# Four modulation vectors summed on VectorE in 128 half chunks; the first gather between expert steps

## The chip, the cores and the metric

The kernel runs on one core of a Trainium2 chip. The time is the device time of one execution in microseconds. Before the change three runs gave a median of 3161.8 us (3160.68 to 3172.74).

## The reference

Two transformer blocks over 256 tokens of width 2048, batch 1, all in float32. Only the first touches the change:

```python
c_act = jax.nn.silu(c)
mod = c_act @ w_ada[l] + b_ada[l]                      # [1, 6 * 2048]
shift1, scale1, gate1, shift2, scale2, gate2 = jnp.split(mod, 6, axis=-1)
h = modulate(rms_norm(x, norm_mix_g[l]), shift1, scale1)
...                                                    # y_sb, y_s5, y_ml: three branches of h
merged = sigmoid(g_sb) * (y_sb @ p_sb) + sigmoid(g_s5) * (y_s5 @ p_s5) + sigmoid(g_ml) * (y_ml @ p_ml)
x = x + gate1[:, None, :] * (merged @ w_out[l])
h = modulate(rms_norm(x, norm_moe_g[l]), shift2, scale2)
x = x + gate2[:, None, :] * hierarchical_moe(h, ...)   # 32 experts, 2 per token
```

The six vectors of 2048 are products of one row, c_act, with a 2048 x 12288 matrix: 96 MB are read for them, and each element is used once. shift1 and scale1 are wanted first of all, gate1 at w_out, shift2 and scale2 after it, gate2 in the experts. The second block (three branches, gates, an output projection) has no such vectors.

## The kernel before

**Chunks.** Weights come in chunks of 128 x 2048 floats (1 MB) from a list `main` of 317, in the order of `PHASES`: p_sb, g_sb, glu, g_sb2, p_s5, g_s5, mlif, ml, p_ml, g_ml, wout, router, then the second block's, which ends in g_c, wout2, ple and pgate. SyncE's queue loads chunk n into one of four slots of `stage`. ScalarE copies it, rounded, to `w_hi` (`high`, line 1302 on), GpSimd subtracts to get `w_lo` (`low`, line 542 on, four instructions of 512 columns, two buffers, so at most two chunks ahead of TensorE), and TensorE forms x_hi w_hi + x_lo w_hi + x_hi w_lo in one of four PSUM banks of `acc`. A chunk of a gate stage (g_*) is `both`: 16 matmuls over 512 columns and 16 over 256; one of a p stage or glu is `half`, one of wout `deep`. ScalarE's `step` waits for the chunk, evacuates it and makes the w_hi four chunks on. In a gate stage the evacuation is a sum of two halves on VectorE, a sigmoid on ScalarE, then one or two multiplications and additions on VectorE (`merge_g`).

**The modulation vectors.** The first two are made at the start (`ada_part`, 32 chunks through `stage`). The other four, numbered u = 0 to 3, ride along: the chunks of `ada` are loaded by ScalarE's queue into one `side_buf` of 1 MB (`side_load`), and after each chunk of g_sb, g_sb2 (u = 0), g_s5 (1), g_ml (2) and wout (3) TensorE waits for the side chunk and multiplies it with c_act as weights: four matmuls of 32 x 512 in four row groups (`side`, `beside_ada`), accumulating in banks 2 or 3 of `wk`. ScalarE loads the next when `side_used` says that this one is done (`side_next`). After 16 chunks it copies 512 columns to `side_row`, TensorE turns them into columns with four matmuls (`ada_columns`), and VectorE adds the bias (`modulation`). An fp32 matmul is two load and two matmul records in the trace.

**The experts.** 192 chunks of 1 MB go through a ring of 8 slots. TensorE gathers the tokens of the first eight teams' slots with 16 tiles of products (`gather(0, ...)`, four matmuls a tile, two PSUM banks), which ScalarE copies to `xg` and `xgo` (`rows_in`), and waits for all 16. Only then comes the first `up_step`, which uses tiles 0 to 3 and ring slots of four experts and gives these back; `up_step(0, c)` uses tiles 4c to 4c + 3.

Everything is in order on its engine, and engines wait for one another by semaphores only.

Of the kernel before, what the change touches and what calls it, by code (L numbers as in the profile page):

```python
# [22 lines left out]
P = 128  # L23
# [70 lines left out]
for _name, _n in VECS:  # L94
    VC[_name] = NV
    NV += _n


def slot(a, i=0, per=1):

    return a % 4, a // 4 + i * per


def build(nc, dr):
# [183 lines left out]
    side_in = nc.alloc_semaphore("side_in")  # L288
# [276 lines left out]
    def _(pe):  # L565
# [171 lines left out]

        def beside_ada(name, u, step, t0=0, n=16):
            for t in range(n):
                k, q = slot(BASE[name] + t)  # L740
                step(k, q)
                side(u, t0 + t)
# [72 lines left out]
        beside_ada("g_sb", 0, both, 0, 8)  # L815
# [190 lines left out]
        gather(0, range(DT))  # L1006
        for d in range(TRIPLES):
            a, b, o = 3 * d, 3 * d + 1, 3 * d + 2
            pe.wait_ge(xg_ready, DT * (d + 1))
            if d:  # L1010
                pe.wait_ge(hid_ready, a - 1)
            up_step(a, 0)
            if d:
                combine(b - 3)
            up_step(a, 1)
            if d:
                down_step(o - 3, 0)
            up_step(a, 2)
            if d:
                down_step(o - 3, 1)  # L1020
            up_step(a, 3)
            if d:
# [270 lines left out]
    def _(act):  # L1293
        def fn(o, i, f, **kw):
            return act.activation(o, i, f, **kw)  # L1295
# [42 lines left out]
        def side_load(u, t):  # L1338
            act.dma_start(side_buf[u][:], dr["ada"][NADA + u * 16 + t]).then_inc(side_in, 16)

        def side_next(u, t):
            act.wait_ge(side_used, u * 16 + t + 1)
            if t < 15:
                side_load(u, t + 1)
            else:
                fn(side_row[u][:], wk[:, 2 + u % 2, :], ACT.Copy).then_inc(row_ready, 1)
# [95 lines left out]
        def merge_p(p, pt):  # L1442
            def go(k, q, t):
                step(k, q, lambda: fn(pt[:, ds(t * 2, 2), :] if not isinstance(t, int) else pt[:, 2 * t:2 * t + 2, :],
                                      acc[:, k, :], ACT.Copy).then_inc(evac_done, 1))
            each(act, BASE[p], 8, go)

        def merge_g(g, sg, b2=None, u=None, t0=0, n=16):
# [8 lines left out]
            if u is None:  # L1457
                each(act, BASE[g], 16, go)
            else:
                for t in range(t0, t0 + n):  # L1460
                    go(*slot(BASE[g] + t - t0), t)
                    side_next(u, t)
            sg_n[0] += n

        act.wait_ge(y5_ready, 9)
        side_load(0, 0)
# [4 lines left out]
        merge_g("g_sb", A["sg"], u=0, n=8)  # L1471
        for t in range(4):
            k, q = slot(BASE["glu"] + t)
            if t >= 2:
                act.wait_ge(glu_ready, t - 1)
            step(k, q, to(A["y5sg"][:, t % 2, :], k, ACT.Sigmoid, 2))
        act.wait_ge(glu_ready, 4)
        fn(yh[:], A["y5"][:], ACT.Copy).then_inc(gelu_done, 1)
        merge_g("g_sb2", A["sg"], u=0, t0=8, n=8)
        act.wait_ge(sg_used, 16)  # L1480
        merge_p("p_s5", ptmp1)
        act.wait_ge(ada_sum, 3)
        side_load(1, 0)
        merge_g("g_s5", A["sg"], u=1)


# [52 lines left out]
        side_load(2, 0)  # L1539
        merge_p("p_ml", ptmp1)  # L1540
        merge_g("g_ml", B["sg"], u=2)
        side_load(3, 0)
# [10 lines left out]
        for t in range(16):  # L1553
            wout_step(*slot(BASE["wout"] + t), t, t < 13)
            side_next(3, t)
# [298 lines left out]
    def _(dve):  # L1854
        def tt(o, a, b, op):
            return dve.tensor_tensor(o, a, b, op)  # L1856
# [228 lines left out]

        def merge_g(g, sg, pt, first=False, t0=0, n=16):
# [4 lines left out]
            def go(k, q, t):  # L2091
# [3 lines left out]
                tt(sg[:, k % 2, :], sg[:, k % 2, :], acc[:, k, T:2 * T], ADD).then_inc(sg_sum, 1)  # L2095
                dve.wait_ge(evac_done, q * 4 + k + 1)
# [7 lines left out]
            if n < 16:  # L2104
                for t in range(t0, t0 + n):
                    go(*slot(BASE[g] + t - t0), t)
            else:
                each(dve, BASE[g], 16, go)
            if not first:
                sg_n[0] += 16  # L2110

        dve.wait_ge(gelu_done, 2)
        tt(yl[:], A["y5"][:], yh[:].bitcast(F32), SUB).then_inc(y_split, 1)
        merge_g("g_sb", A["sg"], ptmp1, True, 0, 8)
        for t in range(4):
            dve.wait_ge(evac_done, BASE["glu"] + t + 1)
            o = A["y5"][:, 2 * t:2 * t + 2, :]
            tt(o, o, A["y5sg"][:, t % 2, :].rearrange("p (c t) -> p c t", c=2), MUL).then_inc(glu_ready, 1)
        dve.wait_ge(gelu_done, 3)
        tt(yl[:], A["y5"][:], yh[:].bitcast(F32), SUB).then_inc(y_split, 1)  # L2120
        merge_g("g_sb2", A["sg"], ptmp1, True, 8, 8)
        modulation(2)
        merge_g("g_s5", A["sg"], ptmp1)
# [84 lines left out]
        stage_b(None, 3)  # L2208
        merge_g("g_ml", B["sg"], ptmp1)
# [13 lines left out]
        modulation(4)  # L2223
        dve.wait_ge(mod_ready, 5)
        stt(a2[:], mod[:, 64:80], 1.0, vec[:, VC["g_moe"]:VC["g_moe"] + 16], ADD, MUL).then_inc(mod_ready, 1)
        each(dve, BASE["wout"], 16, add_out)
# [687 lines left out]
```

## Time and profile before

| | us |
|---|---|
| median of three runs | 3161.8 |
| lowest and highest | 3160.68, 3172.74 |
| the profiled execution's own time | 3177.29 |
| its span, first to last instruction | 3175.4 |
| TensorE, VectorE, ScalarE, GpSimd busy | 2880.4, 1291.5, 1189.0, 1687.4 |

The profile is one execution. Its rows give, by engine or group, the busy time, the mean of one instruction, and how long the engine stood idle before it and for whom. PE is TensorE's matmuls, PEld its weight loads, DVE VectorE, ACT ScalarE, POOL GpSimd, SPq and ACTq the queues from which DMAs are issued.

### The profile page before, as it was taken

What the parts mean: (1) busy time and instruction counts of PE and PEld (TensorE: products, weight loads), DVE (VectorE), ACT (ScalarE), POOL (GpSimd) and SP (SyncE); (2) the same over time, 40 slices, a digit from 0 to 9 for tenths busy, and PEclk for the clock granted to TensorE, in tenths of its full rate; (3) what the DMA queues carried; (4) which work ended last, traced back from release to release, by engine and by line L of the source; (5) the groups of instructions that cost most, each with busy time, mean ns of one, the idle gap of its engine ahead of it and who ended that gap; (6) DMA issues with size and microseconds to landing.
All of it is one profiled execution on the core that took longest, in us unless ns stands there. A gap on an engine that the chain in (4) does not pass through costs nothing.

```text
span 3175.4 us, 51257 instructions
## 1 busy us (share of the span) xinstructions
PE 2880.4 (91%) x19812; PEld 2380.7 (75%) x19812; DVE 1291.5 (41%) x2025; ACT 1189.0 (37%) x1457; POOL 1687.4 (53%) x1274
## 2 busy tenths in 40 slices
PE   6899989999999999858788879889999999999998
PEld 1688777787998778733343338789988989998998
DVE  1488833224544252331222224247723253315344
ACT  1233343333454432321011104556744446644344
POOL 0000067777785875400000004967779997779798
PEclk8999989999999999979998988999999999999999
DMA  9533336667343686549999972534445554435443
GB/s 390 207 129 114 124 133 252 240 253 279 136 162 127 229 299 243 215 186 397 421 397 392 397 310 89 190 138 142 151 146 185 185 189 159 158 144 188 162 165 141
DMA packets 98628, 679.76 MB, mean 214 GB/s; under 512 B 11584, under 2 KB 15424, under 8 KB 16832
## 3 DMA queue, kind: packets, MB, share of 16 engines
q1 hardware_dynamic: 83088, 602.97, 50.3%
q10 hardware_dynamic: 15408, 74.85, 6.4%
q8 instruction: 105, 1.72, 0.2%
q14 instruction: 27, 0.22, 0.0%
HBM read 770.05 MB, written 2.10 MB: 243 GB/s over the span
## 4 chain that ended last, share of the span: by engine, by line
PE 54%; DMA 9%; POOL 4%; DVE 3%; issue 3%; ACT 2%; SPq 1%; ACTq 0%; POOLq 0%; DVEq 0%
PE acc L567 33%; PE wk L567 7%; PE acc L640 7%; DMA ring<-in_moe 6%; POOL w_lo L549 4%; PE acc L644 4%; DMA side_buf<-in_ada 2%; PE acc L653 2%; SPq L499 1%; ACT w_hi L1295 1%; DMA stage<-in_main 1%; DVE hb L1856 0%; DVE dl L1856 0%; ACT L1295 0%; ACT hb L1295 0%
## 5 line engine op out<-in xcount | busy, mean ns | idle before, releaser
L549 POOL TENSOR_TENSOR w_lo<-stage,w_hi 128x512 fp32r<-128x512 f32 x1268 | 1680.2, 1359 | 1439.6 <-ACT w_hi L1295 958.5
L1295 ACT ACTIVATE w_hi<-stage 128x2048 fp32r<-128x2048 f32 x317 | 604.0, 1907 | 49.1 <-DMA stage<-in_main 48.8
L567 PE MATMUL acc<-xhl,w_hi 128*128 128x256 f32 x4064 | 523.7, 287 | 20.9 <-DVE xhl L1856 10.0
L567 PEld LDWEIGHTS acc<-xhl,w_hi 128*128 128x128 f32 x4064 | 507.1, 195 | 24.9 <-DVE xhl L1856 7.5
L640 PE MATMUL acc<-xhl,w_hi 128*128 128x512 f32 x1536 | 373.7, 396 | 0.0
L640 PEld LDWEIGHTS acc<-xhl,w_hi 128*128 128x128 f32 x1536 | 283.5, 189 | 93.9 <-issue 36.7
L567 PE MATMUL acc<-xhl,w_lo 128*128 128x256 f32 x2032 | 271.5, 287 | 2.0 <-POOL w_lo L549 2.0
L567 PEld LDWEIGHTS acc<-xhl,w_lo 128*128 128x128 f32 x2032 | 256.3, 194 | 5.4 <-issue 2.5
L567 PE MATMUL acc<-h,stage 128*128 128x256 f32 x1024 | 234.8, 385 | 2.9 <-ACT h L1295 2.9
L567 PEld LDWEIGHTS acc<-h,stage 128*128 128x128 f32 x1024 | 193.0, 191 | 40.3 <-issue 15.1
L644 PEld LDWEIGHTS acc<-xhl,w_lo 128*128 128x128 f32 x1536 | 196.9, 191 | 7.5
L644 PE MATMUL acc<-xhl,w_lo 128*128 128x256 f32 x1536 | 199.1, 283 | 0.0
L1295 ACT ACT_TABLE_LOAD x136 | 174.5, 1283 | 50.9 <-DVE G_sg L1856 27.4
L567 PE MATMUL acc<-ring,xg 128*32 128x512 f32 x1024 | 135.3, 673 | 51.1 <-DMA ring<-in_moe 49.2
L1862 DVE SCALAR_TENSOR_TENSOR x<-wk,mod,x 128x256 f32<-128x256 f32 x192 | 82.4, 480 | 185.6 <-PE wk L567 185.5
L567 PEld LDWEIGHTS acc<-ring,xg 128*32 128x32 f32 x1024 | 36.4, 121 | 140.5 <-issue 136.0
L567 PE MATMUL acc<-yh,w_hi 128*128 128x256 f32 x576 | 139.8, 281 | 0.0
L567 PE MATMUL acc<-yl,w_hi 128*128 128x256 f32 x576 | 139.6, 281 | 0.0
L567 PE MATMUL acc<-dh,w_hi 128*128 128x256 f32 x512 | 126.8, 288 | 6.4 <-DVE dl L1856 6.4
L1295 ACT ACTIVATE X_ysb<-wk 128x2048 f32<-128x2048 f32 (+1 forms) x12 | 22.5, 1878 | 283.6 <-PE wk L567 187.7
L567 PE MATMUL acc<-dl,w_hi 128*128 128x256 f32 x512 | 124.9, 284 | 0.0
L567 PEld LDWEIGHTS acc<-dh,w_hi 128*128 128x128 f32 x512 | 98.2, 192 | 19.3 <-issue 16.2
(486 smaller groups left out, 4021.6 us busy)
## 6 DMA issues: line engine op xcount, KB each, us to landing
stage<-in_main SPq DMA_DIRECT2D x317, 1024.0 KB, 4.8
ring<-in_moe SPq DMA_DIRECT2D x192, 1024.0 KB, 10.6
side_buf<-in_ada ACTq DMA_DIRECT2D x64, 1024.0 KB, 5.0
over_lo<-in_moe ACTq DMA_DIRECT2D x48, 1024.0 KB
over_hi<-in_moe ACTq DMA_DIRECT2D x42, 1024.0 KB
stage<-in_ada SPq DMA_DIRECT2D x32, 1024.0 KB, 8.6
stage<-in_sb SPq DMA_DIRECT2D x32, 1024.0 KB, 4.8
x<-in_x ACTq DMA_DIRECT2D x1, 2048.0 KB, 12.9
```

Of the source, the lines that this page charges most:

```text
L499: sp.dma_start(ring[:, r, :], dr["moe"][tile * 6 + c]).then_inc(ring_in[r], 16)
L549: last = pool.tensor_tensor(w_lo[:, k % 2, cs], stage[:, k, cs], w_hi[:, k, cs].bitcast(F32), ALU.subtract)
L567: return pe.matmul(o, w, r, start=start, stop=stop)
L640: pe.matmul(acc[:, k, :], w_hi[:, k, t * P:(t + 1) * P], xhl[:, :, t, :], start=t == 0, stop=False, skip_group_check=True)
L644: last = pe.matmul(acc[:, k, 0:T], w_lo[:, k % 2, t * P:(t + 1) * P], xh[:, t, :], start=False, stop=t == DT - 1, skip_group_check=True)
L653: return pe.matmul(o, w, r, start=start, stop=stop, skip_group_check=True)
L1295: return act.activation(o, i, f, **kw)
L1862: return dve.scalar_tensor_tensor(out=o, in0=a, scalar=s, in1=b, op0=op0, op1=op1)
```

## The change

The four side vectors leave TensorE. Each `ada` chunk is loaded as two halves of 128 x 1024 floats (512 KB) into two buffers, and VectorE multiplies a half with c_act's column (a scalar per partition) and adds it to 1024 columns of `wk` in PSUM (`side_sum`), 128 times. `SIDE` says how many halves go with each chunk of each stage: 32 for each vector, u = 0 over p_sb to g_sb2, 1 over p_s5 and g_s5, 2 over p_ml and the first eight of g_ml, 3 over the last four of g_ml and wout. After the 32nd, ScalarE copies all 2048 columns, and TensorE sums over the partitions with 16 matmuls of 128 x 128 weights by one column of ones (`side_columns`), after the first chunk of p_s5, after mlif, after the tenth chunk of g_ml and after wout. In the expert stage the first gather's tiles 8 to 11 stand behind tiles 0 to 7 and the first up_step, tiles 12 to 15 behind the second. In the diff the three engines' parts are put under their names.

```diff
+SIDE = {"p_sb": (1, 1, 2, 1, 2, 1, 2, 2), "g_sb": (1,) * 8, "glu": (1,) * 4, "g_sb2": (1,) * 8,
+        "p_s5": (0, 0, 2, 2, 2, 2, 2, 2), "g_s5": (2, 1, 1, 1) * 4,
+        "p_ml": (2,) * 8, "g_ml": (2,) * 8 + (0, 0, 0, 0, 1, 2, 1, 2), "wout": (2,) * 12 + (1, 1, 0, 0)}
...
+def side_halves(name, t):
+    return range(SIDE_FROM[name][t], SIDE_FROM[name][t + 1])
...
-    side_at = [S0 + 14336, S0 + 14336, S0 + 12288, XH0]
-    side_buf = [sb(f"side_buf{u}", [P, CH], at=at) for u, at in enumerate(side_at)]
-    side_row = [sb(f"side_row{u}", [P, 512], at=at) for u, at in enumerate(side_at)]
+    side_at = [S0 + 14336, S0 + 14336, S0 + 12288, S0 + 12288]
+    side_buf = [sb(f"side_buf{u}", [P, 2, CH // 2], at=at) for u, at in enumerate(side_at)]
+    side_row = [sb(f"side_row{u}", [P, CH], at=at) for u, at in enumerate(side_at)]
...
@@ TensorE
-        def side(u, t):
-            pe.wait_ge(side_in, 16 * (u * 16 + t) + 16)
-            ada_part(side_buf[u], t, 2 + u % 2).then_inc(side_used, 1)
+        def side_columns(u):
+            v = 2 + u
+            pe.wait_ge(row_ready, v + 1)
+            for b in range(16):
+                last = mm(wk[:, 1, v * 16 + b:v * 16 + b + 1], side_row[u][:, b * P:(b + 1) * P], ones[:, 0:1])
+            last.then_inc(ada_sum, 1)
...
-        beside_ada("g_sb2", 0, both, 8, 8)
+        each(pe, BASE["g_sb2"], 8, both)
         pe.wait_ge(y_split, 2)
-        each(pe, BASE["p_s5"], 8, half)
-        ada_columns(2, side_row[0])
-        beside_ada("g_s5", 1, both)
+        half(*slot(BASE["p_s5"]))
+        side_columns(0)
+        for t in range(1, 8):
+            half(*slot(BASE["p_s5"] + t))
+        each(pe, BASE["g_s5"], 16, both)
         each(pe, BASE["mlif"], 1, wide)
-        ada_columns(3, side_row[1])
+        side_columns(1)
...
-        beside_ada("g_ml", 2, both)
+        for t in range(16):
+            both(*slot(BASE["g_ml"] + t))
+            if t == 9:
+                side_columns(2)
...
             deep(*slot(BASE["wout"] + t))
-            if t == 1:
-                ada_columns(4, side_row[2])
-            side(3, t)
-        ada_columns(5, side_row[3])
+        side_columns(3)
...
-        gather(0, range(DT))
+        for c in range(4):
+            gather(0, range(4 * c, 4 * c + 4))
+            if c:
+                pe.wait_ge(xg_ready, 4 * c)
+                up_step(0, c - 1)
+        pe.wait_ge(xg_ready, DT)
+        up_step(0, 3)
...
@@ ScalarE
+        def side_load(n):
+            b, cs = n % 2, slice(n % 2 * (CH // 2), (n % 2 + 1) * (CH // 2))
+            act.dma_start(side_buf[n // 32][:, b, :], dr["ada"][NADA + n // 2][:, cs]).then_inc(side_in[b], 16)
+        def side_first(u):
+            for b in range(2):
+                side_load(u * 32 + b)
+        def side_next(name, t):
+            for n in side_halves(name, t):
+                act.wait_ge(side_used, n + 1)
+                if n % 32 < 30:
+                    side_load(n + 2)
+                if n % 32 == 31:
+                    fn(side_row[n // 32][:], wk[:, :, :].rearrange("p a b -> p (a b)"), ACT.Copy).then_inc(row_ready, 1)
...
@@ VectorE
+        def side_sum(name, t):
+            for n in side_halves(name, t):
+                b = n % 2
+                o = wk[:, 2 * b:2 * b + 2, :].rearrange("p a b -> p (a b)")
+                c = cact[:, n // 2 % 16:n // 2 % 16 + 1]
+                dve.wait_ge(side_in[b], 16 * (n // 2) + 16)
+                if n % 32 < 2:
+                    if n >= 32:
+                        dve.wait_ge(mod_ready, n // 32 + 2)
+                    ts(o, side_buf[n // 32][:, b, :], c, MUL).then_inc(side_used, 1)
+                else:
+                    dve.wait_ge(side_used, n - 1)
+                    stt(o, side_buf[n // 32][:, b, :], c, o, MUL, ADD).then_inc(side_used, 1)
...
                 tt(sg[:, k % 2, :], sg[:, k % 2, :], acc[:, k, T:2 * T], ADD).then_inc(sg_sum, 1)
+                if g in SIDE:
+                    side_sum(g, t - t0)
                 dve.wait_ge(evac_done, q * 4 + k + 1)
```

In p_sb, glu, p_s5, p_ml and wout `side_sum` and `side_next` are called after each chunk in the same way; `modulation(4)` and `a2` move from before wout to after the tenth g_ml chunk, `side_first(1)` waits for the columns of vector 0, and `side_first(3)` for those of vector 2.

## Rows read from the trace of the kernel before

**Rows 1.** The page: busy time and share of each engine.
```profile
PE 2880.4 (91%) x19812; PEld 2380.7 (75%) x19812; DVE 1291.5 (41%) x2025; ACT 1189.0 (37%) x1457; POOL 1687.4 (53%) x1274
```

**Rows 2.** Busy time by stretch (columns in the first row): two of block one, one of block two.
```profile
core 0: us, PE busy (x) PEld busy (x) DVE busy (x) ACT busy (x) POOL busy (x), PEclk, DMA share, GB/s
466.69:770.72 304.03, 287.88 (x1868) 235.43 (x1870) 95.36 (x112) 109.33 (x94) 235.47 (x176) 0.98 0.70 256
1067.27:1305.06 237.79, 228.10 (x1599) 187.33 (x1597) 79.64 (x82) 72.39 (x66) 169.33 (x129) 0.99 0.75 275
2859.52:3052.05 192.53, 189.09 (x1363) 178.59 (x1362) 76.28 (x81) 78.37 (x69) 169.30 (x128) 1.00 0.50 176
```

**Rows 3.** The same of g_s5, g_b and p_b; then groups by line in g_s5.
```profile
656.40:763.10 106.70, 100.33 (x608) 77.98 (x606) 46.20 (x54) 33.74 (x30) 80.27 (x61) 1.00 0.79 286
2500.50:2584.10 83.60, 83.60 (x498) 74.51 (x497) 43.93 (x53) 34.96 (x30) 80.62 (x61) 1.00 0.53 188
2455.00:2494.70 39.70, 39.70 (x323) 39.05 (x322) 4.05 (x6) 16.66 (x14) 35.68 (x28) 1.00 0.51 186
...
L549 POOL TENSOR_TENSOR w_lo<-stage,w_hi 128x512 fp32r<-128x512 f32 x61 | 81.5, 1367 | 27.0 <-PE acc L644 25.7 <-PE acc L567 1.3
...
L640 PEld LDWEIGHTS acc<-xhl,w_hi 128*128 128x128 f32 x224 | 41.0, 188 | 19.0 <-issue 10.9
```

**Rows 4.** The tile side_buf: duration min/median/max, waits for it, landing.
```profile
L567 PE MATMUL wk<-side_buf,cact x512: 592/616/1062, 477.8 to 1313.1; 128*32 128x512 f32 x171
L1339 ACTq DMA_DIRECT2D side_buf<-in_ada x64: 334/334/357, 432.3 to 1306.9; - x64
...
  DMA side_buf<-in_ada: 52.0, 44
...
DMA to landing us min/median/max: 4.6/5.0/7.6
```

**Rows 5.** Timeline at the end of wout: start, length, engine, operation, [idle before].
```profile
1314.44 0.97 PEld L567 LDWEIGHTS wk<-ident,side_row 128*128 128x128 f32 x8 [1.62 <-ACT side_row L1295]
...
1315.32 6.78 PEld L567 LDWEIGHTS acc<-ident,ones 128*128 128x128 f32 x60
...
1325.50 0.30 PEld L567 LDWEIGHTS wk<-rms_red,ones 128*128 128x128 f32 x2 [3.40 <-DVE rms_red L1868]
```

**Rows 6.** Groups by line and shape: VectorE's, then ScalarE's from the page.
```profile
L1862 DVE SCALAR_TENSOR_TENSOR x<-wk,mod,x 128x256 f32<-128x256 f32 x192 | 82.4, 480 | 185.6 <-PE wk L567 185.5
...
L1856 DVE TENSOR_TENSOR A_sg<-A_sg,ptmp 128x256 f32<-128x256 f32 x16 | 22.0, 1374 | 10.5 <-ACT A_sg L1295 10.5
...
L1856 DVE TENSOR_TENSOR merged<-merged,A_sg 128x256 f32 x16 | 21.0, 1311 | 2.0
...
L1856 DVE TENSOR_TENSOR A_sg<-A_sg,acc 128x256 f32<-128x256 f32 x32 | 13.5, 421 | 1.1
...
L1856 DVE TENSOR_TENSOR x<-x,R_ot 128x256 f32 x16 | 16.9, 1059 | 82.5 <-ACT R_ot L1295 82.5
...
L1856 DVE TENSOR_TENSOR hb<-x,rinv 128x1024 f32<-128x1024 f32 x8 | 9.3, 1220 | 0.1
L1856 DVE TENSOR_TENSOR hb<-merged,rinv 128x1024 f32<-128x1024 f32 x4 | 9.1, 2340 | 0.0
...
L1295 ACT ACTIVATE w_hi<-stage 128x2048 fp32r<-128x2048 f32 x317 | 604.0, 1907 | 49.1 <-DMA stage<-in_main 48.8
```

**Rows 7.** DMA issues between 1290 and 1450 us: count, KB each, median us to landing.
```profile
R_iota<-in_iota ACTq DMA_DIRECT2D x1, 128.0 KB, 2.2
```

**Rows 8.** Timeline of the first gather and expert steps; a stretch of the expert stage.
```profile
1384.03 0.38 ACT L1295 ACTIVATE xg<-acc 128x256 f32<-128x256 f32 x1 [0.17 <-PE acc L567]
...
1391.08 0.16 PEld L567 LDWEIGHTS acc<-ring,xg 128*32 128x32 f32 x8 [0.96 <-ACT xgo L1295]
...
1394.79 40.45 SPq L499 DMA_DIRECT2D ring<-in_moe  x20
...
1450.00:1550.00 100.00, 86.08 (x623) 41.72 (x616) 23.14 (x64) 15.41 (x38) 0.00 (x0) 0.97 0.98 402
```

More of the change, by code:

```diff
@@ L96 @@
     NV += _n
+SIDE = {"p_sb": (1, 1, 2, 1, 2, 1, 2, 2), "g_sb": (1,) * 8, "glu": (1,) * 4, "g_sb2": (1,) * 8,
+        "p_s5": (0, 0, 2, 2, 2, 2, 2, 2), "g_s5": (2, 1, 1, 1) * 4,
+        "p_ml": (2,) * 8, "g_ml": (2,) * 8 + (0, 0, 0, 0, 1, 2, 1, 2), "wout": (2,) * 12 + (1, 1, 0, 0)}
+SIDE_FROM, _n = {}, 0
+for _name, _per in SIDE.items():
+    SIDE_FROM[_name] = [_n + sum(_per[:j]) for j in range(len(_per) + 1)]
+    _n += sum(_per)
+assert _n == 128
+def side_halves(name, t):
+    return range(SIDE_FROM[name][t], SIDE_FROM[name][t + 1])
 def slot(a, i=0, per=1):
@@ L287, in build @@
     ada_used = nc.alloc_semaphore("ada_used")
-    side_in = nc.alloc_semaphore("side_in")
+    side_in = [nc.alloc_semaphore(f"side_in{b}") for b in range(2)]
     side_used = nc.alloc_semaphore("side_used")
@@ L736, in _ @@
         ada_columns(1, ada_row[:, 1, :])
[L738 to L742, printed above, removed]
         def stage_a(g, s):
@@ L1445, in go, with merge_g @@
                                       acc[:, k, :], ACT.Copy).then_inc(evac_done, 1))
-            each(act, BASE[p], 8, go)
-        def merge_g(g, sg, b2=None, u=None, t0=0, n=16):
+            if p not in SIDE:
+                each(act, BASE[p], 8, go)
+                return
+            for t in range(8):
+                go(*slot(BASE[p] + t), t)
+                if t == 1 and p == "p_s5":
+                    act.wait_ge(ada_sum, 3)
+                    side_first(1)
+                side_next(p, t)
+        def merge_g(g, sg, b2=None, t0=0, n=16):
             n0 = sg_n[0] - t0
@@ L1456, in go @@
                 step(k, q, evac)
-            if u is None:
+            if g not in SIDE:
                 each(act, BASE[g], 16, go)
             else:
-                for t in range(t0, t0 + n):
-                    go(*slot(BASE[g] + t - t0), t)
-                    side_next(u, t)
+                for t in range(n):
+                    go(*slot(BASE[g] + t), t0 + t)
+                    side_next(g, t)
+                    if t == 10 and g == "g_ml":
+                        act.wait_ge(ada_sum, 5)
+                        side_first(3)
             sg_n[0] += n
         act.wait_ge(y5_ready, 9)
-        side_load(0, 0)
+        side_first(0)
         merge_p("p_sb", ptmp1)
@@ L1470, in _ @@
         fn(yh[:], A["y5"][:], ACT.Copy).then_inc(gelu_done, 1)
-        merge_g("g_sb", A["sg"], u=0, n=8)
+        merge_g("g_sb", A["sg"], n=8)
         for t in range(4):
@@ L1538, in _ @@
         act.wait_ge(by_ready, 4)
-        side_load(2, 0)
+        side_first(2)
         merge_p("p_ml", ptmp1)
-        merge_g("g_ml", B["sg"], u=2)
-        side_load(3, 0)
+        merge_g("g_ml", B["sg"])
         def wout_step(k, q, t, more=True):
@@ L1554, in _ @@
             wout_step(*slot(BASE["wout"] + t), t, t < 13)
-            side_next(3, t)
+            side_next("wout", t)
         rms_root(2)
@@ L2102, in go @@
                     tt(merged[:, t, :], merged[:, t, :], sg[:, k % 2, :], ADD).then_inc(sg_used, 1)
-            if n < 16:
-                for t in range(t0, t0 + n):
-                    go(*slot(BASE[g] + t - t0), t)
+            if g in SIDE:
+                for t in range(n):
+                    go(*slot(BASE[g] + t), t0 + t)
+                    if t == 9 and g == "g_ml":
+                        modulation(4)
+                        scale2()
             else:
@@ L2110, in merge_g @@
                 sg_n[0] += 16
+        for t in range(8):
+            side_sum("p_sb", t)
         dve.wait_ge(gelu_done, 2)
@@ L2118, in _ @@
             tt(o, o, A["y5sg"][:, t % 2, :].rearrange("p (c t) -> p c t", c=2), MUL).then_inc(glu_ready, 1)
+            side_sum("glu", t)
         dve.wait_ge(gelu_done, 3)
@@ L2122, in _ @@
         modulation(2)
+        for t in range(8):
+            side_sum("p_s5", t)
         merge_g("g_s5", A["sg"], ptmp1)
@@ L2208, in _ @@
         stage_b(None, 3)
+        for t in range(8):
+            side_sum("p_ml", t)
         merge_g("g_ml", B["sg"], ptmp1)
@@ L2222, in _ @@
         split_merged(1)
[L2223 to L2226, printed above, removed]
+        for t in range(16):
+            add_out(*slot(BASE["wout"] + t), t)
+            side_sum("wout", t)
         dve.wait_ge(ot_used, 16)
```

34 lines of the change are left out of this document (12 added, 22 removed).

## The prediction, made before the change was run

> **What bounds the kernel now.** I read the first part of the page, then the stretches of the two blocks side by side, then the side buffer's tile, then the groups of VectorE. TensorE is busy for 91% of the span, GpSimd for 53%, VectorE for 41% [rows 1]; work that stays beside TensorE costs time only where it delays it. The second block does the work of the first without side chunks, so it shows what the first could cost. One chunk is four w_lo instructions on GpSimd, so the instruction counts of a stretch count its chunks. The first block's 44 chunks from g_sb to the end of g_s5 took 304.0 us (x176), its g_ml and wout 237.8 us (x129, 32 chunks); the second block's g_c and wout2, the same 32 chunks, took 192.5 us (x128) [rows 2]. In g_b 15 chunks take 83.6 us, 5.57 each, TensorE busy throughout and GpSimd for 80.6 us of it; in p_b 7 half chunks take 39.7 us, 5.67 each. In g_s5 the same 15 chunks take 106.7 us, 7.11 each, at the full clock: 1.54 us more per chunk. TensorE and GpSimd are both near the limit at 5.57: GpSimd in g_s5 idles for 27.0 us, waiting for TensorE [rows 3].
>
> The 1.54 us are the side step: its matmuls (8 records a chunk of 616 ns median, four at a time, about 1.1 us), 52.0 us of idle time waiting for the one side buffer (44 times), and a gap of issue behind each, 10.9 us in g_s5 alone [rows 3, 4].
>
> **Part 1, the matmuls leave TensorE.** If the g and wout stages fall to the second block's pace: 32 gate chunks x 5.573 + 12 half chunks x 5.671 = 246.4 us in place of 304.0, a gain of 57.6; g_ml and wout 192.5 in place of 237.8, a gain of 45.3. The small transposes of ada_columns (0.97 us each [rows 5]) are in these stretches twice and go with them; the third, after mlif, goes against its replacement.
>
> **Part 2, the column sums.** Each of four vectors now wants 16 matmuls of 128x128 weights by one column, in place of 4. One fp32 matmul is two records: the 4 gave x8 loads in 0.97 us, and 60 loads of the same kind took 6.78 us, 0.12 each [rows 5]. So 32 x 0.12 = 3.9 us per vector; the upper bound is 6.1, if each load stood alone for 0.19. Three lie on TensorE in stretches that it bounds: 3.9 behind the first p_s5 chunk, 3.9 in g_ml, 3.9 - 1.0 = 2.9 behind mlif. The fourth stands before the spinning matmuls at the end of wout, where TensorE then waits 3.4 us for the squares [rows 5]; it costs nothing there. The row copies grow from 512 to 2048 columns (1.9 us by the w_hi copy, as long [rows 6]); ScalarE makes each one chunk or more before TensorE asks. Two waits are new: after the tenth g_ml chunk VectorE (modulation(4)) and, one chunk on, ScalarE (its next side load) wait for the column sums. Behind them stand the copies and the evacuation of the chunk that TensorE begins only then, 5.6 us before they are due. After g_s5 both engines waited for mod in the same places before. SP's and GpSimd's programs don't change.
>
> **Part 3, the sums on VectorE.** 128 instructions over 1024 columns, SBUF and PSUM in, PSUM out. No such row exists. Nearest below: PSUM and SBUF in with a pointer scalar, 256 columns, 480 ns; with 1.04 ns per further column (421 ns at 256, 1220 at 1024) this gives 1.28 us. Upper bound: operations with two SBUF inputs are stretched beside a working GpSimd, at 1024 columns from 1220 to 2340 ns, at 256 from 421 to about 1374. With one input in PSUM they stay at 421 beside the same GpSimd [rows 6], so I take 1.28 and keep 2.34 for the range. Lower bound: 1.22.
> The Trainium skill, "SBUF — State Buffer", section "SBUF: two separate sides", has a lock behind this: a VectorE operation with two SBUF inputs and a GpSimd operation exclude one another for whole instructions. By its rule the new sums, with one SBUF input, are free of it; the trace agrees for SBUF output (421 against 1374 ns), and none here writes PSUM.
> VectorE per chunk of g_s5 is 0.42 + 0.42 + 1.37 + 1.31 = 3.5 us [rows 6]; with 1.25 sums on average 5.1, below 5.57. In wout 1.06 + 2.56 = 3.6 against 6.5. In the first eight g_ml chunks, two sums each, it is 6.1, with gaps about 6.4 against 5.57: VectorE falls 0.8 behind per chunk, 6.4 us in all, then catches up in the four chunks without sums. What waits for it is ScalarE's sigmoid, then the next w_hi behind it on ScalarE; GpSimd asks for that w_hi two chunks later (11.1 us), so about 8 us of lateness cost nothing. But p_ml already hands over some. I charge half, 3 us.
>
> **Part 4, the side loads.** 128 loads of 512 KB in two buffers in place of 64 of 1024 KB in one, each issued by ScalarE (0.33 us) after the sum that frees its buffer. Landing: 128 KB took 2.2 us, 1024 KB 5.0 (4.6 to 7.6) [rows 4, 7]; in between, 3.4. A loop of sum, issue and landing is 1.28 + 0.35 + 3.4 = 5.0 us, and a chunk with two halves uses each buffer once: 5.0 to 5.6 per chunk. This just fits under 5.57. Behind the wait for the sum on ScalarE stand the next evacuation and w_hi (1.9 us [rows 6]), both inside the landing time. Of the first eight g_ml chunks this asks 2 MB per 5.57 us, 376 GB/s; g_s5 ran at 286 GB/s with a DMA share of 0.79 [rows 3], the experts at 402 with 0.98 [rows 8]. It is close to full for 36 chunks at most. I charge nothing beyond the 3 us, and keep the rest for the rival.
> The Trainium skill, "DMA: Bandwidth & Descriptors", section "Bandwidth", wants transfers of at least 1 MiB, since each pays a fixed part of about 2 us ("Anatomy of one DMA"): halving pays that twice. As an estimate from this page a half is 2.0 + 1.2 = 3.2 us, the loop 4.8, and the sum stays. It speaks against the change only if the loop, not TensorE, is the bound; the trace's 2.2 us for 128 KB agrees with a fixed part of about that size.
> In p_sb (12 halves), p_s5 (12) and p_ml (16) VectorE has almost nothing else, and ScalarE's step, mostly its w_hi, fits in the landing time. At the end of p_sb the last two sums come before ScalarE's Gelu and the split: about 2 us later, and the first gate chunk's w_hi with it. I charge 2.
>
> **Part 5, the first gather.** The expert stage is a stream of DMA, 0.98 of the engines, and it starts when the first expert step gives its four ring slots back. The eighth tile's gather was copied at 1384.03; the first expert matmul started at 1391.08 behind the sixteenth, and the first refill was issued at 1394.79, 3.7 us later [rows 8]. Now the step starts behind the eighth gather: 1383.95 + 3.7 = 1387.7, 7.1 us earlier. The second step (four gathers at half of 1391.08 - 1384.03, 3.5 us, and 3.7 for itself) ends by 1394.9, before the four new chunks have landed (10 us at 402 GB/s), so the stream has no hole, and the whole of it moves forward by 7.1. Bounds: 4 us if the second step left a hole of 3, 8 if the two gathers ran at the faster pace of the later ones. pick_rows(1) and the first over_load move later by two steps and by the code are wanted only behind the fourth.
>
> **The sum.** 57.6 - 3.9 + 45.3 - 3.9 - 2.9 + 7.1 = 99.3. Less 3 (VectorE in g_ml), 2 (Gelu), and 2.5 because the stretches with a mean clock of 0.98 and 0.99 may keep half of their slow part, which the second block's do not have: 92. The profiled execution took 3177.3 us, so 3085 in its own time; the median of the runs is 15.5 below it, so 3161.8 - 92 = 3070.
>
> **Rivals.**
> A, VectorE becomes the bound: the sums take 2.34 us, as two SBUF inputs would. For it: no row writes PSUM from VectorE. g_s5 is then 3.5 + 2.9 + gaps = 6.75 per chunk (+1.2 x 16 = 19), g_ml's first eight 8.5 (+23), its last four +7, p stages +8: the gain falls by 57 to 35, 3127.
> B, the side loop is the bound: under load a half lands in 6 us, as whole ones did at 7.6 at worst [rows 4]. A two-half chunk is then 7.7 us: p_s5 +12, p_ml +9, g_ml +17, wout +15 = 53, gain 39, 3123. For it the 376 GB/s; against it the median of 5.0 for twice the bytes.
> C, slower: each sum holds GpSimd off for its whole length. Place: the w_lo instructions, of which four take 4 x 1.367 = 5.5 us of a chunk's 5.57 [rows 3], so nothing hides it. 128 x 1.28 = 164 us against the 99 gained: 3161.8 + 65 = 3227. It decides from 99 / 128 = 0.78 us per sum. Against it: the 421 ns rows, where nobody waited.
> D, the pace of the first block has another cause than the side step and stays near 6.9: then only the gather and a few us of waits remain, 3150. Against it: the same chunks at 5.57.
>
> **Chances.** Forecast 0.64 (its own range 3052 to 3092), A 0.08, B 0.15, D 0.06, C 0.07. A change of 0.5% (16 us) is what a measurement of this kernel can tell from none. The forecast, A and B are faster: 0.87; D is the same: 0.06; C slower: 0.07. The range 3048 to 3128 holds the forecast, A and B.
>
> **What would show it.** Right: g_s5 and g_ml near 5.6 us per chunk and wout near 6.5, the sums at about 1.28 us, w_lo still at 1.37, side_columns at about 3.9, the halves landing in 3.4 to 4.5, the first refill 3.7 us behind the eighth gather. Wrong: w_lo waiting for ScalarE or running over 1.5 us, sums over 2 us, or VectorE waiting for the side loads in most two-half chunks.

## The result, and the profile after

The changed kernel took 3133.3 us (median of five runs, 3129.39 to 3143.89), the kernel before 3162.6 beside it: a ratio of 0.9898, 95% interval 0.9883 to 0.9914. It is faster by 29 us; 92 were forecast and the forecast was 3070. Rival B, the side loop bound by its landings, had given 3123.

The page's first row and the two stretches of [rows 2] in the kernel after (columns as there). The first stretch runs again from the first w_lo of g_sb to that of mlif, the second from the first of g_ml to the router's:

```profile
PE 2828.8 (90%) x19396; PEld 2393.7 (76%) x19396; DVE 1415.8 (45%) x2153; ACT 1194.6 (38%) x1457; POOL 1679.5 (54%) x1274
```

```profile
466.04:723.92 257.88, 254.92 (x1654) 233.93 (x1653) 142.63 (x164) 113.21 (x95) 231.96 (x176) 0.99 0.83 290
1024.33:1261.30 236.97, 207.53 (x1408) 192.31 (x1407) 129.06 (x134) 75.79 (x66) 165.77 (x129) 0.94 0.75 261
...
1024.33:1145.85 121.52, 100.64 (x543) 87.01 (x542) 72.80 (x85) 41.48 (x36) 84.16 (x64) 0.90 0.72 252
1145.85:1261.30 115.45, 106.89 (x867) 105.29 (x866) 56.27 (x50) 34.31 (x30) 81.61 (x65) 0.97 0.78 270
```

The same change, two answers. The first stretch fell from 304.0 us to 257.9 [rows 2], most of what was forecast. The second stayed: 237.8 to 237.0. TensorE is busy there for 20 us less than before (207.5 against 228.1), and the time went into idling: g_ml alone grew from 111.6 to 121.5, with 20.9 us of TensorE idle in it and a granted clock of 0.90. Against the 92.8 us that the same 16 chunks took without most of the side loads (experiment 3) it is 28.8 longer: 20.9 of idle time, and 7.9 of busy time more (100.6 against 92.8) at the lower grant. The first stretch asks for one half beside most chunks; p_ml, the first eight chunks of g_ml and twelve of wout ask for two.

What was late? The tile side_buf after the change, with how long VectorE stood for its loads, who then stood for VectorE, and the landings (compare [rows 4]):

```profile
L1357 ACTq DMA_DIRECT2D side_buf<-in_ada x128: 334/334/528, 431.7 to 1258.5; - x128
...
  DMA side_buf<-in_ada: 181.3, 72
...
  ACT R_ot L1312: 54.4, 11
  ACT ptmp L1312: 53.5, 11
...
DMA to landing us min/median/max: 3.8/5.6/10.2
```

A half of 512 KB landed in 5.6 us (median), where 1024 KB had taken 5.0 [rows 4] and the forecast had 3.4. Half the bytes did not come sooner. The loads of `stage` took longer too: between the first w_lo of g_ml and the router's their median was 6.8 us, in the kernel before 4.8. VectorE waited for 72 of the 128 halves. Neither VectorE's work nor GpSimd's was the trouble, as the groups by line show (the sums; the w_lo copies, 1367 ns in g_s5 in [rows 3]):

```profile
L1894 DVE SCALAR_TENSOR_TENSOR wk<-side_buf,cact,wk 128x1024 f32<-128x1024 f32 x120 | 154.1, 1287 | 161.9 <-DMA side_buf<-in_ada 161.6
...
L564 POOL TENSOR_TENSOR w_lo<-stage,w_hi 128x512 fp32r<-128x512 f32 x1268 | 1672.3, 1352 | 1399.2 <-ACT w_hi L1312 1001.7
```

How a late half reaches TensorE is seen in one chunk of g_ml, in the timeline of VectorE, of ScalarE and its queue, and of GpSimd (start, length, engine, operation, idle before and for whom):

```profile
1057.47 1.29 DVE L1894 SCALAR_TENSOR_TENSOR wk<-side_buf,cact,wk 128x1024 f32<-128x1024 f32 x1 [5.09 <-DMA side_buf<-in_ada]
...
1060.79 0.42 DVE L1888 TENSOR_TENSOR B_sg<-B_sg,acc 128x256 f32<-128x256 f32 x1
...
1063.03 1.29 DVE L1894 SCALAR_TENSOR_TENSOR wk<-side_buf,cact,wk 128x1024 f32<-128x1024 f32 x1 [0.63 <-DMA side_buf<-in_ada]
...
1058.79 0.33 ACTq L1357 DMA_DIRECT2D side_buf<-in_ada  x1
1061.30 0.42 ACT L1312 ACTIVATE B_sg<-B_sg 128x256 f32<-128x256 f32 x1 [6.70 <-DVE B_sg L1888]
1061.62 1.90 ACT L1312 ACTIVATE w_hi<-stage 128x2048 fp32r<-128x2048 f32 x1
...
1063.59 5.38 POOL L564 TENSOR_TENSOR w_lo<-stage,w_hi 128x512 fp32r<-128x512 f32 x4 [3.92 <-ACT w_hi L1312]
```

VectorE stands 5.09 us for a half. Behind that sum, in order, are the four small operations that give ScalarE the next gate's sum; ScalarE had idled for 6.70 us, then makes the w_hi, and GpSimd, idle for 3.92, follows. The load issued at 1058.79 is used at 1063.03, 4.2 us later, and only when that sum is done can the buffer's next load start. The waits of that stretch, and what TensorE stood for:

```profile
ACT B_sg L1312 <- DVE B_sg L1888: 56.5, 13, 10.6
DVE wk L1894 <- DMA side_buf<-in_ada: 32.2, 17, 5.2
POOL w_lo L564 <- ACT w_hi L1312: 25.8, 11, 6.1
...
PE wk L582 <- ACT side_row L1312: 10.7, 1, 10.7
```

The last row is one wait: after its tenth g_ml chunk TensorE asks for the row of u = 2, whose last sum was late. Half of g_ml's idle time is this one place. The column sums behind it (32 records, from 1107.9) took 6.8 us, at a grant of 0.50.

The end of wout, in stretches (the wait for the last row, then the 16 column sums):

```profile
1262.00:1268.40 6.40, 0.14 (x2) 0.00 (x0) 3.59 (x3) 2.34 (x3) 4.42 (x4) 0.68 0.75 230
1268.40:1275.20 6.80, 6.74 (x32) 6.74 (x32) 6.32 (x4) 2.02 (x4) 0.00 (x0) 0.50 1.01 423
```

TensorE idles for 6.4 us, its granted clock falls to 0.50 of 2.4 GHz, which is the 1.2 GHz level, and the sums take 6.8 us, where 3.9 were forecast and four buffers gave 3.5. The gather part came out as forecast. The first expert weights were loaded behind the eighth gather, and the first refill followed 3.7 us later:

```profile
1343.61 0.16 PEld L582 LDWEIGHTS acc<-ring,xg 128*32 128x32 f32 x8 [0.25 <-ACT xgo L1312]
...
1347.32 2.00 SPq L514 DMA_DIRECT2D ring<-in_moe  x4
```

### The profile page after: what moved, and what is told of

It reads as the page before. It is cut to its first block, busy times and chain, and to the rows that moved or that the text cites. A ratio compares the mean times of both kernels' runs of the same rounds, so it can differ in the third digit from the quotient of the medians.

```text
span 3131.4 us, 50496 instructions
## 1 busy us (share of the span) xinstructions
PE 2828.8 (90%) x19396; PEld 2393.7 (76%) x19396; DVE 1415.8 (45%) x2153; ACT 1194.6 (38%) x1457; POOL 1679.5 (54%) x1274
## 4 chain that ended last, share of the span: by engine, by line
PE 68%; DMA 16%; DVE 5%; ACT 4%; POOL 3%; issue 2%; SPq 1%; ACTq 0%; POOLq 0%; DVEq 0%
PE acc L582 43%; PE wk L582 10%; PE acc L655 8%; DMA ring<-in_moe 6%; DMA side_buf<-in_ada 6%; PE acc L659 4%; POOL w_lo L564 3%; DMA stage<-in_ada 2%; PE acc L668 2%; DVE wk L1894 1%; DMA stage<-in_main 1%; ACT w_hi L1312 1%; ACT L1312 1%; SPq L514 1%; ACT hb L1312 0%
## 5 line engine op out<-in xcount | busy, mean ns | idle before, releaser
L564 POOL TENSOR_TENSOR w_lo<-stage,w_hi 128x512 fp32r<-128x512 f32 x1268 | 1672.3, 1352 | 1399.2 <-ACT w_hi L1312 1001.7
L1894 DVE SCALAR_TENSOR_TENSOR wk<-side_buf,cact,wk 128x1024 f32<-128x1024 f32 x120 | 154.1, 1287 | 161.9 <-DMA side_buf<-in_ada 161.6
## 6 DMA issues: line engine op xcount, KB each, us to landing
ring<-in_moe SPq DMA_DIRECT2D x192, 1024.0 KB, 10.7
```

The source lines that it names most:

```text
L564: last = pool.tensor_tensor(w_lo[:, k % 2, cs], stage[:, k, cs], w_hi[:, k, cs].bitcast(F32), ALU.subtract)
L1894: return dve.scalar_tensor_tensor(out=o, in0=a, scalar=s, in1=b, op0=op0, op1=op1)
```

## The experiments

Eleven further kernels ran. A ratio is always to the kernel before, on the same chip, and the medians are of each kernel's own runs. On the chips in question the kernel before had medians from 3162.6 to 3171.2 us, so a difference between the medians of two kernels can hold up to 9 us of the chip; the difference of their ratios is given beside it where it matters. Three theories stand against one another: **latency** (a buffer can be filled again only when its sum is done, and the landing of 4 to 10 us doesn't fit into a chunk with two buffers), **bandwidth** (the engines that move the data are full) and **holding** (ScalarE, standing for the sum before its next copy, is what costs).

**1. The gather alone.** The kernel before, with the first gather between the expert steps as in the diff, and nothing else.

> The kernel before with only the first gather put between expert steps. If the traces' ledger is right (first refill 11.6 us behind the first gather matmul instead of 19.5), the time falls by 7 to 8 us: 3162.6 to about 3155. If the expert stage takes it back later (its end is set by something other than the stream of loads), it stays within 3 us of 3162.6.

3163.55 us beside 3169.28, ratio 0.9982 (0.9967 to 0.9997): 5.7 us. The first refill came 11.5 us after the first gather matmul, in the kernel before 19.5. The interval is 1 to 10 us, so the forecast's 7.1 stands.

**2. The side vectors alone.** The changed kernel with `gather(0, range(DT))` in one piece again.

> The changed kernel with the gather in one piece as before. If the two parts are independent, 3133.3 + 8 = about 3141, so the sums on VectorE are worth about 21 us. If the parts depend on one another (the earlier start collides with something), this run is at 3133 or the two gains do not add up to 29 us.

3137.99 us, ratio 0.991 (0.9894 to 0.9925). The two parts add up: 0.90% here and 0.18% in 1, against 1.02% for the changed kernel. As the gather gave what it should, what the stages gained too little lies in the side vectors.

**3. Each vector's halves loaded once.** The sums and the waits for them stay as many, but only the first two halves of a vector are loaded, so 8 side loads are issued in place of 128; the vectors, and with them the experts' choice of rows, are not the reference's, so only the time up to the router counts.

```diff
             for n in side_halves(name, t):
                 act.wait_ge(side_used, n + 1)
-                if n % 32 < 30:
-                    side_load(n + 2)
...
-                dve.wait_ge(side_in[b], 16 * (n // 2) + 16)
+                dve.wait_ge(side_in[b], 16 * (n // 32) + 16)
```

> The changed kernel, but each vector's two halves are loaded only once and all 16 sums of a buffer read the same data; it leaves out 120 of the 128 side loads, so the vectors are not the reference's. Theory 1 (landing times of the two-buffer loop, with ScalarE held behind it): no wait for a landing is left, gate chunks at 5.6 to 6.3 us, g_ml 95 to 100 us instead of 121.5, time about 3090. Rival (VectorE's occupancy or ScalarE's wait for the sums themselves is what costs): g_ml stays over 115 us, time over 3120.

3114.51 us; the router's first w_lo at 1214.8 in place of 1261.3. The whole missed the 3090 expected behind the router: the expert stage, which works on other rows here, took 504.6 us from the first refill to the last, in the changed kernel 470.4. g_ml:

```profile
1017.08:1109.84 92.76, 92.76 (x561) 82.99 (x560) 70.01 (x78) 39.13 (x34) 84.32 (x64) 1.00 0.55 193
```

TensorE is busy throughout. The sums and ScalarE's wait for them are still all there, so without the transfers neither costs anything that shows. This rules out holding by the sum itself, but not bandwidth.

**4. Four buffers.** The same 128 loads and bytes; u = 1 to 3 have four buffers of 512 KB.

```diff
-    side_at = [S0 + 14336, S0 + 14336, S0 + 12288, S0 + 12288]
-    side_buf = [sb(f"side_buf{u}", [P, 2, CH // 2], at=at) for u, at in enumerate(side_at)]
+    side_bufs = [(S0 + 14336, S0 + 18432), (S0 + 14336, S0 + 18432, S0, S0 + 4096),
+                 (S0 + 12288, S0 + 16384, S0, S0 + 4096), (S0 + 12288, S0 + 16384, S0, S0 + 8192)]
...
-                if n % 32 < 30:
-                    side_load(n + 2)
+                if n % 32 + side_per[n // 32] < 32:
+                    side_load(n + side_per[n // 32])
```

> The changed kernel with four buffers of 512 KB for the second, third and fourth vector (two for the first), same bytes and same order of everything else. Theory 1a (latency of a two-buffer loop): landings of 5.6 us are hidden, g_ml near 100 us, time about 3105. Theory 1b (the DMA engines are full in chunks with two halves, 2 MB per 5.6 us): landings grow with the loads in flight, g_ml stays near 120 us and the time within 5 us of 3133.

3090.49 us (3078.67 to 3095.74), ratio 0.974 (0.9726 to 0.9755), 43 us below the changed kernel by the medians, 50 by the ratios. g_ml and wout in stretches, then the side loads:

```profile
1018.23:1112.57 94.34, 94.34 (x561) 84.17 (x561) 73.81 (x81) 39.67 (x34) 84.33 (x64) 0.98 0.83 311
1112.57:1217.57 105.00, 100.61 (x827) 99.81 (x826) 63.33 (x53) 37.93 (x33) 83.90 (x65) 0.98 0.80 293
```

```profile
  DMA side_buf<-in_ada: 84.6, 30
...
DMA to landing us min/median/max: 3.4/5.8/10.0
```

A half still takes 5.8 us to land, so the transfers are no faster; more of them are in the air, and the rate rises from 252 to 311 GB/s in g_ml. Bandwidth falls: the stretch was not short of it. Latency holds. With 128 loads g_ml is now within 1.6 us of experiment 3, and wout took 105.0 us in both.

**5. Three buffers.** As 4, with three.

> As four buffers, but three buffers of 512 KB for the vectors of p_s5/g_s5, p_ml/g_ml and wout. A half then has about one and a half chunks to land in place of one (two buffers, 3133) or two (four buffers, 3090.5). Landing theory: the halves take 5.8 us with a tail to 10, so a third buffer covers the median and not the tail: most of the 43 us come back, g_ml near 97 to 105 us, total 3095 to 3110. If it was not the depth but something else in the four-buffer kernel (other addresses, other semaphores), three buffers give about what four give, 3090, or nothing, 3133.

3093.09 us, ratio 0.9758 (0.9734 to 0.9782). g_ml took 107.0 us and wout 105.6, with a median landing of 5.9. The total is a little below the 3095 to 3110 of the landing theory and its interval overlaps that of 4, so the totals can't tell three buffers from four. The stage can, in one profile of each: g_ml took 121.5, 107.0, 94.3 us with two, three, four, in the order of the depth.

**6. Issued later, two buffers.** ScalarE's wait for a sum, and the load behind it, stand behind the next chunk's evacuation and w_hi.

```diff
+        def side_later(name, t):
+            while behind:
+                side_next(*behind.pop())
+            if any(n % 32 == 31 for n in side_halves(name, t)) or t + 1 == len(SIDE[name]):
+                side_next(name, t)
+            else:
+                behind.append((name, t))
...
-                side_next(p, t)
+                side_later(p, t)
```

> The changed kernel with its two buffers; only ScalarE's wait for a sum, with the load behind it, is moved behind the evacuation and the w_hi copy of the next chunk. Two theories of the 44 us that the side loop costs against four buffers. Holding theory: what costs is that ScalarE stands in that wait (the wait for the sum in front of the next evacuation and w_hi); then TensorE and GpSimd no longer wait in the gate stages, g_ml falls from 121.5 towards 95 us and the total to about 3095 to 3105. Landing theory: what costs is that a load is issued only when its buffer is free, 5.6 us before its data can be used; then the move issues each load later, VectorE waits for halves for more than the 181 us of before, g_ml stays at 120 or grows to 135, and the total is 3133 to 3160.

3211.35 us, ratio 1.0126 (1.0102 to 1.015): 78 us more than the changed kernel (72 by the ratios) and slower than before. It is outside even what the landing theory gave, on its side. g_ml in one stretch; then VectorE's wait for the halves and the landings:

```profile
1063.38:1214.67 151.29, 107.92 (x561) 93.46 (x560) 66.20 (x84) 41.35 (x36) 81.86 (x65) 0.82 0.59 206
```

```profile
  DMA side_buf<-in_ada: 299.1, 85
...
DMA to landing us min/median/max: 3.5/5.4/11.9
```

The median landing didn't grow (5.4 against 5.6), but each load starts later, and the wait rises from 181 to 299 us. The edit moves ScalarE's wait and the load together, so what it shows is the loop: made longer by a copy of 1.9 us and what stands before it, it costs more, and freeing ScalarE did not make up for it. Holding was ruled out by 3, and finds no support in 7.

**7. Issued later, four buffers.** The edit of 6 on the kernel of 4.

> Four buffers, and ScalarE's wait for the sum behind the next chunk's evacuation and w_hi. With four buffers the load has the slack to be late. Landing theory: little is left for ScalarE's order to give, within 6 us of the 3090.5 of four buffers. Holding theory: the waits that are left in g_ml and in g_s5 (94 and 89 us for 16 chunks against 83.6 for 15 in g_b) are ScalarE's, so another 5 to 12 us go, 3078 to 3085.

3098.3 us, ratio 0.9779 (0.976 to 0.9799): the same edit that cost 78 us with two buffers costs 8 with four (12 by the ratios). Much of that can lie where the depth is still two: u = 0 kept its two buffers, and g_sb, which it rides along, took 7.0 us longer than in 4 (56.6 against 49.6), while g_ml took 96.4 against 94.3 and wout 104.9 against 105.0. With the depth to cover it, lateness of an issue hardly matters.

**8. Whole blocks in DRAM.** With two buffers, each half is stored by itself, so that a row of 4 KB lies beside the next, in place of a gap of 4 KB between them.

```diff
-            act.dma_start(side_buf[n // 32][:, b, :], dr["ada"][NADA + n // 2][:, cs]).then_inc(side_in[b], 16)
+            act.dma_start(side_buf[n // 32][:, b, :], dr["ada_half"][n]).then_inc(side_in[b], 16)
```

> The changed kernel with its two buffers; the two halves of each side chunk lie as separate 512 KB blocks in DRAM, in place of 4 KB pieces with gaps of 4 KB between them. Sharing theory: a half takes 5.6 us (median) because it flies beside a 1 MB stage load and the other half, so nothing changes: median 5.4 to 5.8 us, total 3125 to 3140. Stride theory: the gaps make the transfer slow; then the median falls to 4 us or below, the two-buffer loop fits under a chunk, and the total falls to about 3095 to 3110.

3114.3 us, ratio 0.9821 (0.9803 to 0.9838), clear of the changed kernel's 0.9898, and as neither of its two theories had it: the median landing is 5.4, as sharing said, but the total is below its 3125. Its landings, then g_ml and wout:

```profile
DMA to landing us min/median/max: 3.0/5.4/9.9
```

```profile
1021.91:1142.67 120.76, 103.23 (x561) 89.86 (x560) 74.78 (x85) 41.45 (x36) 84.50 (x65) 0.90 0.69 253
1142.67:1255.14 112.47, 106.74 (x872) 105.75 (x870) 58.48 (x51) 34.40 (x31) 82.39 (x65) 0.97 0.78 284
```

g_ml is unchanged. By the router the profiled execution is 6 us ahead of the changed kernel's, of the 19 between the medians (24 by the ratios). It was the slowest of its five, 3124.0 us and so 9.7 above its median; where the rest is from, these profiles don't show, and why the layout should matter stays open. The expert stage, the same work in each, took 465.1 us here and 470.4 in the changed kernel.

**9. Whole blocks and four buffers.**

> Four buffers with the halves as separate 512 KB blocks in DRAM. With two buffers the separate blocks gave about 19 us (0.9821 against 0.9898 of before), because the loop there pays for every tenth of a microsecond. If that is the whole of it, four buffers have little left to give: 3082 to 3092, g_ml near 93 us. If the 4 KB pieces cost by themselves (they take time from the stage loads too), 15 to 20 us go again: 3070 to 3076, and p_ml and wout get shorter.

3083.45 us (3080.45 to 3084.91), ratio 0.9734 (0.9714 to 0.9754), the best here, but its interval holds that of 4. With the depth there, the layout is worth nothing that these runs can tell.

**10. Loads of 256 KB.** Two buffers, every side load but a vector's first two brings half of its columns; the vectors are not the reference's, and again only the time up to the router counts.

```diff
-            b, cs = n % 2, slice(n % 2 * (CH // 2), (n % 2 + 1) * (CH // 2))
+            b, w = n % 2, CH // 2 if n % 32 < 2 else CH // 4
+            cs = slice(n % 2 * (CH // 2), n % 2 * (CH // 2) + w)
```

> The changed kernel with two buffers, where every side load but a vector's first two brings 256 KB in place of 512 KB (the second half of each buffer keeps older data, so the vectors aren't the reference's and the expert stage does other work: what counts is the time up to the router). Issues, waits and sums are the same in number. Sharing theory: the landing is mostly the bytes at their share of the engines, so the median falls from 5.6 to 3.5 to 4 us, and with it the loop: g_ml 121.5 to 95, the router's first w_lo at 1215 to 1225 in place of 1261. Fixed-cost theory: a load pays most of its time however small it is, then the median stays at 4.8 or more and g_ml at 110 to 120, the router at 1245 or later.

The router's first w_lo was at 1235.9, between the 1225 of one theory and the 1245 of the other. Landings and g_ml:

```profile
DMA to landing us min/median/max: 3.0/4.3/10.2
```

```profile
1020.96:1130.12 109.16, 99.05 (x561) 87.82 (x560) 69.88 (x83) 39.10 (x34) 84.89 (x64) 0.92 0.64 221
```

Half the bytes took the median from 5.6 to 4.3. g_ml gave back 12 of the 27 us that four buffers gave there, and by the router it was 25 of 44. VectorE still waited for its halves for 126 us, against 181 with full loads and 85 with four buffers. So smaller loads are a weaker cure than more buffers, and this one also moves half of the bytes.

**11. Column sums twice.** The kernel of 4, with `for b in list(range(16)) * 2` in `side_columns`.

> Four buffers, and each of the four groups of 16 column-sum matmuls is done twice, with the same values. The prediction's step: 3.9 us a group in three places on TensorE's path, none in the fourth, where TensorE waits for the squares: 11.7 us over four buffers, about 3102. If the groups hide in slack of the stages they stand in: 0 to 4 us, about 3092. If the waits behind them (VectorE's modulation, ScalarE's next side load) carry on: 15 to 25 us, about 3110.

3111.65 us, ratio 0.9807 (0.9789 to 0.9825): 21 us more than four buffers, where 11.7 followed from the forecast. In the profiled executions it is behind by 6.3 us at the first w_lo of mlif (one extra group), by 12.1 at that of p_ml (two) and by 20.7 at that of wout (three). Of this 0.7 stood before g_sb and 3.4 came in p_ml, which has no group; the stretches with the groups grew by 5.6, 5.7 and 5.3 us. The fourth adds 7.5 from the start of the squares to the rms matmul (19.2 against 11.7), where the single group had been hidden. The price is mostly in the groups: from its first matmul to the next other one a single group took 4.5, 3.5, 3.5 and 3.5 us, a doubled one 9.7, 9.4, 8.7 and 10.6. The kernel of 4 first, around its first group (before it, with it, behind it, and later), then the same with two:

```profile
583.00:591.50 8.50, 8.50 (x67) 8.19 (x66) 4.04 (x6) 4.73 (x4) 8.15 (x7) 1.00 0.70 266
592.50:597.00 4.50, 4.15 (x31) 4.15 (x31) 0.00 (x0) 2.58 (x3) 4.42 (x4) 0.83 0.63 233
597.00:609.00 12.00, 12.00 (x83) 12.00 (x83) 0.18 (x1) 2.40 (x2) 3.90 (x4) 0.78 0.45 140
...
609.00:621.00 12.00, 12.00 (x104) 12.00 (x103) 6.50 (x6) 4.56 (x4) 10.75 (x10) 1.00 1.00 372
```

```profile
593.50:604.00 10.50, 10.50 (x71) 10.50 (x70) 0.07 (x1) 2.81 (x3) 5.32 (x5) 0.73 0.56 201
604.00:616.00 12.00, 12.00 (x85) 12.00 (x86) 0.37 (x2) 2.40 (x2) 4.05 (x4) 0.81 0.24 77
```

The grant is 1.00 until the column sums, 0.83 in the stretch with them and 0.78 in the 12 us of ordinary matmuls behind them, where 83 are done in place of 104; then 1.00 again. With the group doubled it is 0.73 and 0.81, and TensorE has no idle time in either stretch, nor anywhere in g_ml (99.6 us, all busy). So it is not the waits behind the groups, though their theory had the total right with its 3110. In the kernel before, p_s5 had no such group in it and ran at 1.00 from its first w_lo to that of g_s5; in the changed kernel this stretch ran at 0.93. The lower clock is the rest of the group's price: an extra group cost 5 to 6 us in three places, not 3.9. It did not follow every group: in experiment 3 the 12 us behind the third group ran at 1.00.

## Why the prediction was wrong

**The step that failed** is Part 4: "in between, 3.4" for the landing, the loop of 5.0 that "just fits under 5.57", and "I charge nothing beyond the 3 us". The 3.4 lay between 128 KB at 2.2 us and 1024 KB at 5.0. But the 2.2 was one load in a quiet stretch [rows 7], and the 5.0 had one side load in the air at a time; now there are two, beside a stage load of 1 MB that itself takes 4.8 over the whole kernel and 6.8 in g_ml and wout. The median was 5.6 and the loop 1.29 + 0.33 + 5.6 = 7.2 us, with landings up to 10.2. A chunk of two halves uses each buffer once, so where every chunk has two, it can't on average be shorter than that loop. The third vector (u = 2, two halves a chunk throughout) bears it out: the first and the last sum on one of its buffers started at 992.1 and 1102.1 us, 15 turns of 7.3 us. And not only the median counts, since VectorE, ScalarE and GpSimd hand each late half on, as the one chunk above shows.

Rival B had the mechanism (6 us a landing, 7.7 per chunk) at a chance of 0.15. Its places came out in part: beside four buffers, p_ml and g_ml together took 30.9 us longer (26 charged) and wout 10.5 (15 charged), but p_s5 and g_s5 together only 0.4 (12 charged), and the 6 us between the router and the first gather it did not name. Its size was near, a gain of 39 where the profiled executions show 44, but in part by luck, as the places show. Its evidence, the 7.6 at worst in [rows 4], should have weighed more than a median taken from another load.

Set beside the stages, in us of the profiled executions (each from the first w_lo of a stage to that of the next, the last three by the first gather matmul and the first refill):

| stretch | before | forecast | after | four buffers | issued later |
|---|---|---|---|---|---|
| g_sb to g_s5 | 304.0 | 250.3 | 257.9 | 256.9 | 283.0 |
| mlif to p_ml | 296.6 | 299.5 | 300.4 | 295.1 | 312.7 |
| g_ml to the first gather | 308.0 | 266.6 | 311.4 | 267.6 | 351.9 |
| of it g_ml | 111.6 | | 121.5 | 94.3 | 151.3 |
| to the first refill | 19.5 | 12.4 | 11.6 | 12.4 | 11.4 |
| to the end | 1780.6 | 1780.6 | 1784.1 | 1795.7 | 1779.2 |

The forecast column is the sum's terms without its 7.5 us of deductions, which is about what g_sb to g_s5 missed (7.6). Only one cell of "after" is far off, by 44.8, and with four buffers it is within one.

- **Part 1**, the matmuls leave and the pace falls to the second block's: right where the halves are on time. g_sb to g_s5 fell by 46.1 of the forecast 53.7 with two buffers; all of it together, to the first refill, by 96.6 with four buffers against 91.8 forecast; that it is more is in part the slow start of the kernel before's profiled execution (below). Rival D is out.
- **Part 2**, 3.9 us a group: right for the group at full clock (3.5 in three of the four with four buffers, 4.5 in the first) and too small where the clock was lower, 5 to 6 for an extra group in 11 and 6.8 for the two that came behind idle time in the changed kernel. The fourth group "costs nothing there": wrong in the changed kernel, since the row it needs was late. From the last wout matmul to the rms matmul it took 23.1 us in place of 13.0: the squares' result was late itself, 19.4 us behind that matmul, and TensorE then came 3.7 behind the squares. With four buffers it took 13.0 again, and the group was hidden.
- TensorE's wait for a row had been costed at nothing, because ScalarE makes each "one chunk or more before TensorE asks". After the tenth g_ml chunk it came 10.7 us late, after the last wout chunk 6.3. VectorE's new wait for the column sums was small, as forecast: 2.0 us in g_ml.
- **Part 3**, 1.28 us a sum: 1.287 measured. Rivals A and C are out: w_lo stayed at 1352 ns. The Trainium skill, "SBUF — State Buffer", section "SBUF: two separate sides", frees an operation with one SBUF input from the lock; the trace agrees, now for a PSUM output too, at 1287 ns beside a busy GpSimd.
- The Trainium skill, "DMA: Bandwidth & Descriptors", section "Bandwidth", spoke against halving the loads, and it was weighed only by the fixed part of a single one. The estimate of 3.2 us for a half, worked out in the prediction from the section "Anatomy of one DMA" of the same page, which has its fixed part for loads issued by GpSimd and not by ScalarE as here, is below even the shortest landing, 3.8 us; the median of 5.6 is beside other traffic.
- **Part 5**, 7.1 us: 5.7 alone in 1 (interval 1 to 10), and 7.9 in the stage table.
- **Own time against median**: the 15.5 us that were carried over did not carry. The changed kernel's profiled execution took its median. The profiled execution of before was slow by itself: experiment 1 has the same program up to the first gather and its last wout matmul began at 1305.8, not 1312.5. That accounts for 6.7 of the 15.5; the rest is not traced. Without this term the forecast would have been missed by 48 us, not 63.

The miss of 63.3 us adds up: 44.3 before the first refill (47.5 gained, 91.8 forecast), 3.5 behind it, 15.5 of own time against median.

What stays open: with four buffers the medians differ by 79 us, while the profiled executions differ by 96.6 at the first refill. 6.7 of this is before's own slow start. From the first refill to the last, its expert stage took 477.7 us (476.3 in experiment 11), where before took 470.6 and experiment 9, with the same buffers, 467.9; one profile for each kernel can't tell chance from cause.

## What to carry to other kernels

A load that is issued when its buffer comes free needs as many buffers as its landing *under this stretch's traffic*, with its tail, is long in steps; take the landing from rows that share the stretch, not by size from a quiet one. Here a third buffer gave nearly all that four gave in the total, and about half of it in g_ml. Count the loop by buffer and compare it with the step at its densest place, not on the average. And when an execution's own time stands above the median, forecast the difference, and don't carry the excess over as a constant.

## What the runs showed of the hardware

- Landing under load followed the size only weakly (medians): 1024 KB 5.0 us (one in flight), 512 KB 5.6 (two), 256 KB 4.3 (two), 128 KB 2.2 in a quiet stretch. With three and four in flight 512 KB took 5.9 and 5.8 (6.5 in experiment 7), while the rate in g_ml rose to 311 GB/s.
- 16 matmuls of one column, amid full ones, were in most places followed by a lower grant: 1.00, then 0.83 and 0.78, with hardly any idle time of TensorE; behind the third group of experiment 3 it stayed at 1.00. Behind 6.4 us of idle time the same 32 weight loads ran at 0.50 and took 6.8 us in place of 3.5.
- A VectorE sum of PSUM and SBUF into PSUM over 1024 columns took 1.27 to 1.29 us, whatever GpSimd did.
